# Two transformer blocks in split precision on one core: the high-weight products of the up and gate panels as one 512-column matmul per slice instead of two of 256

## The reference

```
x = x + jnp.square(jax.nn.relu(hn @ mlp_w1[l])) @ mlp_w2[l]                    # 1024 -> 4096 -> 1024

def swiglu(x, w_gate, w_up, w_down):                                            # 1024 -> 2816 -> 1024, twice
    return (jax.nn.silu(x @ w_gate) * (x @ w_up)) @ w_down
h = h + 0.5 * swiglu(rms_norm_2(h, ffn1_norm[l]), ffn1_w_gate[l], ffn1_w_up[l], ffn1_w_down[l])
```

## Time and profile before

| | |
|---|---|
| profiled execution | 1017.64 us, of it 1015.8 us from the first to the last instruction |
| mean granted TensorE clock | 0.995 |
| TensorE matmuls busy | 997.7 us (98%), 7106 of them |
| VectorE busy | 607.5 us (60%) |
| ScalarE busy | 491.1 us (48%) |
| median of the three runs | 1014.34 us |

### The profile page before, as it was taken

The page is one execution under the profiler, slowest core; times in us unless marked ns, Lnnn a source line. Parts: engine busy times, 40 slices in busy tenths (PEclk is TensorE's granted clock), DMA queues, the critical chain, the costliest instruction groups (busy, mean ns, idle before and its releaser), DMA issues.

```text
span 1015.8 us, 17060 instructions
## 1 busy us (share of the span) xinstructions
PE 997.7 (98%) x7106; PEld 932.9 (92%) x7106; DVE 607.5 (60%) x755; ACT 491.1 (48%) x611; POOL 57.6 (6%) x87
## 2 busy tenths in 40 slices
PE   6999999999999999999999999999999999999997
PEld 6989999998999999999999998998999899999996
DVE  4765676875645554586556656646655765545554
ACT  5675459634544434473434345444563463434342
POOL 4000000000200000021114001000000010000000
PEclk9999899999999999999999999999999999999999
DMA  9754243556555565537665654643324555555541
GB/s 285 230 168 125 84 130 120 195 179 207 186 181 192 174 198 189 183 125 237 205 209 177 212 186 140 208 125 125 118 91 150 183 176 190 185 183 187 183 157 41
DMA packets 128671, 173.13 MB, mean 170 GB/s; under 512 B 3120, under 2 KB 111936, under 8 KB 128624
## 3 DMA queue, kind: packets, MB, share of 16 engines
q1 hardware_dynamic: 127232, 168.56, 51.5%
q0 software_dynamic: 1392, 3.91, 1.3%
HBM read 171.40 MB, written 1.05 MB: 170 GB/s over the span
## 4 chain that ended last, share of the span: by engine, by line
PE 94%; DMA 2%; DVE 2%; ACT 1%; POOL 0%; issue 0%; SPq 0%; POOLq 0%; ACTq 0%; DVEq 0%
PE ps L574 20%; PE ps L576 20%; PE ps L575 20%; PE acc L574 8%; PE acc L575 8%; PE acc L576 8%; DMA raw<-in_w_in 2%; PE acc L955 2%; PE acc L977 1%; PE ps L707 1%; PE acc L963 1%; PE acc L678 1%; PE acc L834 1%; DVE wl L1400 1%; ACT acth L1117 1%; PE acc L690 1%
## 5 line engine op out<-in xcount | busy, mean ns | idle before, releaser
L574 PE MATMUL ps<-acth,wh 128*128 128x256 f32 x1592 | 456.4, 287 | 0.9 <-ACT xs L1272 0.5
L576 PE MATMUL ps<-acth,wl 128*128 128x256 f32 x1592 | 451.7, 284 | 0.0
L575 PE MATMUL ps<-actl,wh 128*128 128x256 f32 x1592 | 451.7, 284 | 0.0
L574 PEld LDWEIGHTS ps<-acth,wh 128*128 128x128 f32 x1592 | 306.7, 193 | 7.9 <-issue 5.4
L575 PEld LDWEIGHTS ps<-actl,wh 128*128 128x128 f32 x1592 | 306.7, 193 | 2.0 <-issue 0.5
L576 PEld LDWEIGHTS ps<-acth,wl 128*128 128x128 f32 x1592 | 306.6, 193 | 0.0
L1405 DVE TENSOR_TENSOR wl<-raw,wh 128x2048 fp32r<-128x2048 f32 x89 | 208.3, 2342 | 118.6 <-ACT wh L1086 118.6
L1086 ACT ACTIVATE wh<-raw 128x2048 fp32r<-128x2048 f32 x88 | 168.3, 1912 | 153.3 <-PE acc L576 79.4
L1080 ACT ACTIVATE wh<-raw 128x2048 fp32r<-128x2048 f32 x69 | 132.0, 1913 | 142.5 <-PE ps L576 116.1
L1400 DVE TENSOR_TENSOR wl<-raw,wh 128x2048 fp32r<-128x2048 f32 x68 | 155.5, 2288 | 39.6 <-ACT wh L1080 35.2
L574 PE MATMUL acc<-wh,midh 128*128 128x512 f32 x304 | 119.0, 391 | 0.1
(11 more groups left out here) (265 smaller groups left out, 1012.1 us busy)
## 6 DMA issues: line engine op xcount, KB each, us to landing
raw<-in_w_in SPq DMA_DIRECT2D x37, 1024.0 KB, 5.4
raw<-in_mlp_w SPq DMA_DIRECT2D x32, 1024.0 KB, 5.3
raw<-in_ffn_w_gate SPq DMA_DIRECT2D x22, 1024.0 KB, 5.4
raw<-in_ffn_w_up SPq DMA_DIRECT2D x22, 1024.0 KB, 5.3
raw<-in_ffn_w_down SPq DMA_DIRECT2D x22, 1024.0 KB, 5.0
raw<-in_w_out SPq DMA_DIRECT2D x8, 1024.0 KB, 4.9
raw<-in_w_up_rnn SPq DMA_DIRECT2D x4, 1024.0 KB, 5.1
raw<-in_cmp_k_w SPq DMA_DIRECT2D x2, 1024.0 KB, 6.7
```

The lines of the kernel that those rows point to most:

```text
L574: nc.tensor.matmul(out_, lh, rh, start=start, stop=False, **kw)
L575: nc.tensor.matmul(out_, lh, rl, start=False, stop=False, **kw)
L576: return nc.tensor.matmul(out_, ll, rh, start=False, stop=stop, **kw)
```

## The change

`acth` and `actl` become the two halves of one tile `actp`, so that slice k of both lies in 512 neighbouring columns. The new `halved_tile` replaces the three matmuls of a slice by two: the high weights against the 512 columns of `actp` (results: high by high in the left half of a bank, high by low in the right half), and the low weights against `acth`, added to the left half. Each half c of a panel has a bank of its own now: `pair01` (the banks `ps[0]` and `ps[1]`) or `pair67` (`ps[6]` and `ps[7]`). The first panel of each feed-forward part is still made of 256-column matmuls, in the left halves alone (`ffn_first`).

The halves have to be summed: ScalarE copies the right halves of a panel into `ffr` or `ffr2` (`right_half`, 512 columns), VectorE adds the left halves (`add_right`, 512 columns) and goes on from there. In the MLP the copy takes the place of the ReLU, which becomes part of the square (`squared`). The next panel into the same bank waits for the sum (`ff_sum`) in the MLP, bank by bank; in a SwiGLU for `ff_gate` and `ff_prod`, as before. The scales are spread into the right half of the bank of `pair01` that is not in use then.

```diff
-        acth = sb("acth", [P, KT, T], F32R)
-        actl = sb("actl", [P, KT, T], F32R)
+        actp = sb("actp", [P, KT, 2, T], F32R)
+        acth, actl = actp[:, :, 0, :], actp[:, :, 1, :]
...
+        ffr = carve(8448, 2, T)
+        ffr2 = carve(8960, 2, T)
+
+        pair01 = ctx.enter_context(nc.psum_tensor("pair01", [P, 2, 512], F32))
         acc4 = ctx.enter_context(nc.psum_tensor("acc4", [P, 4, 512], F32))
-        ps += [acc4[:, i, :] for i in range(4)]
-        ps += [ctx.enter_context(nc.psum_tensor(f"ps{i}", [P, 512], F32)) for i in (6, 7)]
+        pair67 = ctx.enter_context(nc.psum_tensor("pair67", [P, 2, 512], F32))
+        ps = [pair01[:, i, :] for i in range(2)] + [acc4[:, i, :] for i in range(4)] + [pair67[:, i, :] for i in range(2)]
...
+            def halved_tile(n, c, bank):
+
+                h, l = pv(n, KT, wh), pv(n, KT, wl)
+                cs = slice(c * P, (c + 1) * P)
+                for k in range(KT):
+                    nc.tensor.matmul(bank[:, :], h[:, k, cs], actp[:, k].rearrange("p u t -> p (u t)"),
+                                     start=k == 0, stop=False)
+                    last = nc.tensor.matmul(bank[:, 0:T], l[:, k, cs], acth[:, k, :], start=False, stop=k == KT - 1)
...
-            def ffn_up(n, b, norm=None, between=None):
+            def ffn_first(n, pair, norm):
                 for c in range(2):
-                    m = feature_tile(n, KT, c, ps[b][:, c * T:(c + 1) * T], acth, actl, norm)
+                    m = feature_tile(n, KT, c, pair[:, c, 0:T], acth, actl, norm)
+                    if c == 0 and n == ML:
+                        m.then_inc(ff_half, 1)
+                m.then_inc(panel_done, 1)
+
+            def ffn_up(n, pair, summed=None, between=None):
+                for c in range(2):
+                    if summed is not None:
+                        pe.wait_ge(ff_sum, summed + c)
+                    m = halved_tile(n, c, pair[:, c, :])
                     if c == 0 and between is not None:
                         spread(between)
                 m.then_inc(panel_done, 1)
...
-            ffn_up(ML, 0, 1)
+            ffn_first(ML, pair01, 1)
             seed([3], 1)
             with pe.Fori(0, (ML_STEPS - 1) // 3) as i:
                 for m in range(3):
                     n = ML + 1 + 2 * m
                     pe.wait_ge(lo_ready, i * 6 + (n + 1))
 
-                    pe.wait_ge(ff_act, i * 3 + (ML_F + m + 1))
-                    ffn_up(n, 0)
+                    ffn_up(n, pair01, i * 6 + (2 * m + 1))
                     pe.wait_ge(lo_ready, i * 6 + (n + 2))
...
                 split(n0)
-                ffn_up(n0, 0, j)
+                ffn_first(n0, pair01, j)
                 seed([3], j)
                 split(n0 + 1)
-                ffn_up(n0 + 1, 1, None, j)
+                ffn_up(n0 + 1, pair67, None, j)
...
+            def right_half(to, pair):
+                return nc.scalar.activation(to, pair[:, :, T:2 * T], ACT.Copy)
...
             hi(ML + 2)
-            done(ML)
-            nc.scalar.activation(ffa, ps[0][:, :], ACT.Relu).then_inc(ff_act, 1)
             hi(ML + 3)
...
-                    nc.scalar.activation(ffa, ps[0][:, :], ACT.Relu).then_inc(ff_act, 1)
...
+                done(n0 + 1)
+                right_half(ffr2, pair67).then_inc(ff_right, 1)
...
+                        act.wait_ge(panel_done, i * 6 + (n + 1))
+                        right_half(ffr, pair01).then_inc(ff_right, 1)
                         hi_in_loop(i, n + 3)
 
                         act.wait_ge(ff_gate, i * 2 + (f0 - F1_F + m + 2))
                         nc.scalar.activation(ffa, ffg, ACT.Silu).then_inc(ff_act, 1)
+                        act.wait_ge(panel_done, i * 6 + (n + 2))
+                        right_half(ffr2, pair67).then_inc(ff_right, 1)
+                        if not (last and m and n0 == F2):
+                            hi_in_loop(i, n + 4)
                         act.wait_ge(ff_prod, i * 2 + (f0 + m + 2))
                         hidden_hi((m + 1) % 2).then_inc(ff_hi, 1)
                         if not (last and m and n0 == F2):
-                            hi_in_loop(i, n + 4)
                             hi_in_loop(i, n + 5)
 
...
+            def squared(r):
+                flat_ = r.rearrange("p a t -> p (a t)")
+                return nc.vector.scalar_tensor_tensor(ffs, flat_, 0.0, flat_, ALU.max, ALU.mult)
+
+            def add_right(r, pair):
+                return nc.vector.tensor_tensor(r, pair[:, :, 0:T], r, ALU.add)
+
+            dve.wait_ge(ff_half, 1)
+            nc.vector.tensor_copy(ffr[:, 0, :], pair01[:, 0, 0:T]).then_inc(ff_sum, 1)
+            done(ML)
+            nc.vector.tensor_copy(ffr[:, 1, :], pair01[:, 1, 0:T]).then_inc(ff_sum, 1)
             lo(ML + 2)
-            dve.wait_ge(ff_act, ML_F + 1)
-            nc.vector.tensor_tensor(ffs, ffa, ffa, ALU.mult).then_inc(ff_prod, 1)
+            dve.wait_ge(ff_sum, 2)
+            squared(ffr).then_inc(ff_prod, 1)
...
+                    dve.wait_ge(ff_right, i * 3 + (m + 1))
+                    add_right(ffr, pair01).then_inc(ff_sum, 2)
+                    dve.wait_ge(ff_sum, i * 6 + (2 * m + 4))
 
                     dve.wait_ge(ff_lo, i * 3 + (ML_F + m + 1))
-                    nc.vector.tensor_tensor(ffs, ffa, ffa, ALU.mult).then_inc(ff_prod, 1)
+                    squared(ffr).then_inc(ff_prod, 1)
...
+                def product(at_right, at_sum, at_act, at_lo):
+
+                    dve.wait_ge(ff_right, at_right)
+                    add_right(ffr2, pair67).then_inc(ff_sum, 1)
                     dve.wait_ge(ff_act, at_act)
+                    dve.wait_ge(ff_sum, at_sum)
...
+                def gate(at_right, at_sum):
+
+                    dve.wait_ge(ff_right, at_right)
+                    add_right(ffr, pair01).then_inc(ff_sum, 1)
+                    dve.wait_ge(ff_sum, at_sum)
+                    nc.vector.tensor_tensor(two(ffg), ffr, bc2, ALU.mult).then_inc(ff_gate, 1)
...
-                gate(n0 + 1)
+                done(n0)
+                nc.vector.tensor_tensor(two(ffg), pair01[:, :, 0:T], bc2, ALU.mult).then_inc(ff_gate, 1)
```

More of the change, by code:

```diff
@@ L322, in build @@
         ff_gate = sem("ff_gate")
+        ff_right = sem("ff_right")
+        ff_sum = sem("ff_sum")
+        ff_half = sem("ff_half")
         ff_act = sem("ff_act")
@@ L550, in head2, with spread_to @@
                     [vb[:, kt, DH * g:DH * (g + 1)] for kt in range(TT)])
+        def spread_to(j):
+            return ps[TURNED[0]][:, 0:T] if j == 3 else pair01[:, 0, T:2 * T]
         def up_bank(u, c):
@@ L595, in feature_tile @@
                                  ah[:, k, :], al[:, k, :], k == 0, k == kt - 1)
+                return last
+            def halved_tile(n, c, bank):
[5 more added lines that the diff above has]
+                    last = nc.tensor.matmul(bank[:, 0:T], l[:, k, cs], acth[:, k, :], start=False, stop=k == KT - 1)
                 return last
@@ L908, in spread @@
                 for tt in range(TT):
-                    m = nc.tensor.matmul(ps[TURNED[0]][:, tt * P:(tt + 1) * P], cst[:, C_ONES:C_ONES + P], diag[:, tt, :],
+                    m = nc.tensor.matmul(spread_to(j)[:, tt * P:(tt + 1) * P], cst[:, C_ONES:C_ONES + P], diag[:, tt, :],
                                          start=True, stop=True)
@@ L1429, in take_scales @@
                 dve.wait_ge(bc_done, j - 1)
-                link(nc.vector.tensor_copy(scale_bc, ps[TURNED[0]][:, 0:T]))
+                link(nc.vector.tensor_copy(scale_bc, spread_to(j)))
             def norm_lo(j, v):
@@ L1722, in swiglu @@
             def swiglu(n0, f0, meanwhile=None):
-                def product(at_panel, at_act, at_lo):
-                    dve.wait_ge(panel_done, at_panel)
+                def product(at_right, at_sum, at_act, at_lo):
+                    dve.wait_ge(ff_right, at_right)
+                    add_right(ffr2, pair67).then_inc(ff_sum, 1)
                     dve.wait_ge(ff_act, at_act)
+                    dve.wait_ge(ff_sum, at_sum)
                     dve.wait_ge(ff_lo, at_lo)
-                    nc.vector.scalar_tensor_tensor(ffs, ps[1][:, :], 0.5, ffa, ALU.mult, ALU.mult).then_inc(ff_prod, 1)
-                def gate(at_panel):
-                    dve.wait_ge(panel_done, at_panel)
-                    nc.vector.tensor_tensor(two(ffg), two(ps[0][:, :]), bc2, ALU.mult).then_inc(ff_gate, 1)
+                    nc.vector.scalar_tensor_tensor(ffs, ffr2.rearrange("p a t -> p (a t)"), 0.5, ffa, ALU.mult,
+                                                   ALU.mult).then_inc(ff_prod, 1)
+                def gate(at_right, at_sum):
[3 more added lines that the diff above has]
+                    nc.vector.tensor_tensor(two(ffg), ffr, bc2, ALU.mult).then_inc(ff_gate, 1)
                 j = 2 if n0 == F1 else 4
+                r0 = ML_STEPS - 1 if n0 == F1 else ML_STEPS - 1 + 2 * FF_STEPS - 1
```

(8 more changed lines are left out.)

14 lines of the change are left out of this document (6 added, 8 removed).

## The result

The changed kernel takes 1010.35 us (median of 6 runs, 1007.85 to 1010.80) against 1015.28 (6 runs, 1013.87 to 1015.89) for the kernel before, run beside it: ratio 0.9945, 95% interval 0.9934 to 0.9956. It is faster, by 5.6 us where the prediction had 12.7, and it lies above the range of 998.0 to 1008.5. The forecast counted from 1014.34, the median of three runs of the kernel before; with six it is 1015.28, so 0.9 us of the distance to the forecast 1001.6 are the baseline's. The profiled execution took 1010.49 us, its span 1008.7.

A forecast was written before the change was run, and what follows sets the result against it. TensorE's matmul pace was taken to bound the kernel. From the profiled 1017.64 us, minus 12.0 and minus 0.7 gave 1004.9; from the median 1014.34 the same sum gave the forecast 1001.6 us, range 998.0 to 1008.5.

The forecast's parts named there:

- What bounds the kernel: Whole span: TensorE busy 98%, clock granted nearly in full; other engines' work in the feed-forward parts hidden.
- The main term: Up and gate panels: 912 places go from 0.3594 to 0.3463 us, 12.0 us saved.
- paid per matmul, wide or narrow: TensorE's stream: 0.013 us per matmul beside its columns, the same for 256 or 512 columns.
- The wide matmul never settles: Up and gate panels: wide matmul stays at 0.233, pair 0.3528, 6.0 us gained plus 0.7, 1007.6 us; chance 0.16.
- The added work, costed at nothing: Feed-forward parts: 39 us more on VectorE and 25 on ScalarE, hidden behind TensorE's next panel of 5.5 us.
- the least room at the first step: First step of the first SwiGLU: 0.75 us of room left of 1.9 before TensorE wants the bank.
- The wait behind the first MLP panel: Behind the first MLP panel: TensorE finds its bank free, 0.7 us saved; hidden values ready 0.8 us early.
- The slower case: Load of high weights lies open 0.08 us at each of 912 places, 1075 us; chance 0.03.
- The small waits in the middle of a panel: 15 middle-of-panel waits break the stream; with a missed margin 1.5 to 2 us given back, 1003.4 us; chance 0.07.
- Something that the wide form keeps: The 13 ns stay with the wide matmul, 0.235 each; 4.2 + 0.7 us gained, 1009.4 us; chance 0.05.

The follow-up runs named there:

- short loads: Three 256-column matmuls a slice in the changed kernel, weights of 64 columns in middle slices, results of the other 64 features left out: 1000.79 us.
- the grouped kernel: Changed kernel with all 16 wide matmuls of an up or gate panel first, then the 16 narrow ones: 1003.98 us, 0.9878 to the kernel before.
- the one with three narrow matmuls: Changed kernel with the wide matmul undone in seven of eight slices, 256 columns each again: 1014.66 us, 0.9987 to the kernel before.
- Short low weights: Changed kernel with low weights of slices 1 to 6 loaded with 64 columns instead of 128, their other results left out: 1004.68 us.
- short high ones: Changed kernel with high weights of slices 1 to 7 loaded with 64 columns instead of 128, their other results left out: 999.79 us.
- both together: Changed kernel with 64-column high weights in slices 1 to 7 and low weights in slices 1 to 6, other results left out: 1000.75 us.

## Why the prediction was wrong

**What bounds the kernel: right.** TensorE, at an unchanged clock; 6194 matmuls; VectorE and ScalarE close to the forecast busy time, and hidden except at one place.

**The main term: wrong in its sum, and that is the step that failed.** It added a wide matmul's 0.2265 and a narrow one's 0.1198, each read in a stream of its own width, to 0.3463 for a pair; 0.353 was measured. The prediction put 0.013 us as "paid per matmul, wide or narrow", and so a wide one always at 0.2265. The quantity is made of two (the narrow one with short loads): 0.0066 of the 0.013 is simply the price of 256 columns, 0.1133 and not 0.1067, and the wide form pays it twice; the other 0.0066 hangs on the 128 weight columns, by my reading on their load, which sticks out behind a narrow matmul. In a stream of one width a wide one covers its load (0.2267, twice 0.1133). There the forecast pair holds, since both its parts had been read in such streams: 0.347, as the grouped kernel shows. In the alternation it does not: 0.353. The missing 912 x 0.0066 = 6.0 us are most of the gap between 12.7 and 5.6.

**The rival that had the pair.** "The wide matmul never settles" gave 0.3528 per pair and was right by rows that the prediction had in hand: starts 0.23 and 0.24 apart where the width had just changed. The argument against it, that the narrow one behind a wide one is faster by as much, was half true. The narrow one is faster, but by 3 ns (0.1169), and the wide one slower by 9 (0.2361). I took one interval of 0.11 from rows that are rounded to 0.01 us for a settled value. The rival was lucky in its sum as well: it had 0.233 and 0.1198, each 3 ns off, in opposite directions. Its 1007.6 us missed too, by what follows.

**The added work, costed at nothing: wrong in one place.** The new wait in the first SwiGLU cost 1.04 us. The prediction looked for the least room at the first step and found 0.75 us, and there it held. It did not look for stretches where VectorE's own rows were already three times as long as their kind, `midl` 2.20 and a split 6.76 us, which no wait of TensorE betrayed; the room there was 0.58 us. The wait takes two things together: the masks back to back, since it goes when they are set apart, and the added copy and addition, since the kernel before has the masks and no wait. Whether the product would have kept the room by reading PSUM as before, no run shows.

**The down panels: a term that was missing.** In the SwiGLUs a down panel lasts 5.499 us from its first start to the next panel's, against 5.468 before: 22 x 0.031 = 0.7 us. The grouped kernel has 5.468 again, and so has the one with three narrow matmuls. But the alternation alone is not the cause: in the MLP it stands ahead of the down panels too, and they last 5.468 before and after. What makes the difference stays open.

**The wait behind the first MLP panel: right.** TensorE goes on without a gap, answering to the earlier trace rows:

```profile
261.35 0.40 PE L682 MATMUL acc<-mrgh,zero 128*128 128x512 f32 x1
261.59 0.39 PE L612 MATMUL pair<-actp,wh 128*128 128x512 f32 x1
261.82 0.28 PE L614 MATMUL pair<-actp,wl 128*128 128x256 f32 x1
```

The copies, the split, the square and `midl` were in time as well, `midl` done at 266.17 for a down panel that starts at 267.14, 0.97 us of room where 0.8 was forecast; VectorE, answering to the earlier trace rows:

```profile
261.89 2.28 DVE L1435 TENSOR_TENSOR wl<-raw,wh 128x2048 fp32r<-128x2048 f32 x1
264.09 0.69 DVE L1741 SCALAR_TENSOR_TENSOR xs<-arena 128x512 f32<-128x512 f32 x1
265.48 0.69 DVE L1732 TENSOR_TENSOR midl<-xs,midh 128x512 fp32r<-128x512 f32 x1 [0.70 <-ACT midh L1298]
```

**The sum, redone.** The pairs gave back 240 x (0.3600 - 0.3521) + 672 x (0.3600 - 0.3530) = 6.6 us instead of 12.0. (Of the missing 6.0 above, 0.5 come back because three narrow matmuls cost 0.3600 before and not the 0.3594 of the forecast.) With the wait behind the first panel 6.6 + 0.7, less 1.0 (the new wait) and 0.7 (the down panels), is 5.6 us, against 5.5 by the stages and 5.6 by the ratio.

**The other rivals.** The slower case, a load lying open for 0.08 us at each pair, is out. The small waits in the middle of a panel are not there. "Something that the wide form keeps" was right in kind for half of the 13 ns, the price of its columns. Its time of 1009.4 us is the nearest of all, but partly by luck: its wide matmul of 0.235 is close to the measured 0.236, its narrow one of 0.1198 is 3 ns too slow, and it had neither the new wait nor the down panels. The Trainium skill, in "TensorE: Matmul & The Clock Gate", section "Wait — 56ns, not 53.3ns?", has a fixed cost of 2.5 ns per warm matmul; the runs here show none, since 0.2267 is twice 0.1133.

**What stays open.** Why the alternation with whole loads costs 6 ns more than the same matmuls grouped. Short low weights take 7 ns from the pair, short high ones 13, both together 13 and no more; half the changes of width leave 1 ns. The excess needs both the alternation and whole weights, but no run says by what path one matmul's load delays the other. A load that simply sticks out behind the narrow matmul would give 0.347, and is not enough. Whether it is the load at all, or the number of result partitions that goes with it, is not told apart either.

## What to carry to other kernels

A pace read from a stream of one width does not hold in a mix. Where a change makes a mix, look at the rows where the width changes, take the slow ones as seriously as the fast ones, and keep equal widths together: here the order alone was worth as much as the change itself. Before joining matmuls, ask whether their time is columns or goes with the weights, for here only the second part was saved. And look not only at waits but at an engine's rows that are longer than their own kind: they are delays that some cover hides now, and added work can use that cover up. How much cover is left can be read there: the end of the long row against the start of the matmul that needs it.

## What the runs showed of the hardware that was not expected

- At the full granted clock, 256 columns of this type took 0.1133 us (with 64 weight columns) and 512 took 0.2267 (with 128): 0.443 ns per column, without a fixed part.
- With 128 weight columns loaded for each, the 256-column stream ran at 0.1200, with 64 at 0.1133; the rows of the loads themselves last 190 and 134 ns there. The Trainium skill, in "TensorE: Matmul & The Clock Gate", section "LDWEIGHTS (loading the stationary operand)", says that the time of a load goes by its number of columns; the two paces and the rows agree with that in direction.
- A wide and a narrow matmul in turn took 0.353 us, in twos 0.348, grouped 0.347.
- While GpSimd ran its 128x2048 operation on two SBUF operands (4.68 us), a 128x512 operation of VectorE with both operands in SBUF that began during it ended 0.55 to 0.56 us after it, in all 27 cases of the 14 profiles: its row lasts from 1.20 to 4.46 us, by how early it began, where 0.69 is usual. Those with one operand in PSUM kept their 0.69. The Trainium skill, in "GPSIMD Engine Reference", section "1. Specifications", has SBUF interfaces shared with VectorE, and contention with its instructions that have two SBUF inputs. The rows agree in both halves.
- A moving operand in two pieces streams as fast as one in one piece (173.50 us for the MLP with the gap, 173.51 without).
